# Where VectorE evacuates the last block: six weight splits placed ahead of it

## The chip, the cores and the metric

The kernel runs on one core of a Trainium2 chip. The metric is the device time of one execution in microseconds (us). Engines are named as in the profile: PE (TensorE), PEld (its weight loads), DVE (VectorE), ACT (ScalarE), POOL (GpSimd), SP (SyncE, which here only issues DMAs). Each engine runs its own instruction stream in order and waits on semaphores that others raise.

## The reference, cut to what matters

One layer over 512 tokens of width 1024, float32: a mixer (retention and differential attention), a routed mixture of 16 experts with two experts for each token, and a gated embedding. The change lies where the mixture ends and the gated embedding begins:

```python
for gi in range(N_GROUPS):
    sl = slice(gi * EXPERTS_PER_GROUP, (gi + 1) * EXPERTS_PER_GROUP)
    hid = jax.nn.silu(jnp.einsum('td,edf->etf', t, w_gate[sl])) * jnp.einsum('td,edf->etf', t, w_up[sl])
    hid = hid * combine[:, sl].T[:, :, None]       # routing weights, zero for all but two experts
    out = out + jnp.einsum('etf,efd->td', hid, w_down[sl])
...
x = x + out                                        # out as returned by the mixture
gate = jax.nn.sigmoid(rmsnorm(x, norm_ple[i]) @ w_ple_gate[i])
x = x + gate * (p[i] @ w_ple_proj[i])
return rmsnorm(x, norm_final)
```

## The kernel before, in words

The tokens are four tiles of 128 rows. The mixture sorts the 1024 pairs of token and expert by expert and cuts them into blocks of 64 pairs; in this execution there are 23 blocks. For each block POOL gathers the rows, PE multiplies by gate and up weights (L1556), ACT and DVE make the hidden values, PE transposes them and multiplies by the down weights (L1580) into a PSUM bank. DVE copies that bank to SBUF (`evacuate_y`, L1209), and POOL scatters the copy to `y_rows` in HBM (L657 copies a column of row numbers, L677 issues the indirect DMA). The blocks run in a loop; the last block is finished behind the loop by code of its own.

After the mixture comes what the code calls stage 6. SP waits until the scatter of the last block has landed, and then gathers the two expert rows of every token into `yg`, tile by tile, in eight DMAs of 512 KB (L633). DVE waits for the two of tile 0 and adds them, weighted, to the residual `xr` (`stage6_a`, L1242 and L1243). PE transposes the sum (L1610), ACT rounds it to a high part `x2T_hi` (L897), DVE forms the low part `x2T_lo` (L1250), and PE multiplies by the gate weights in three passes (high by high, low by high, high by low: L1296 to L1298). ACT, DVE and SP finish each tile behind PE.

The gate weights themselves are prepared in between. SP loads them as one DMA of 4 MB (`ple_gate_raw`, L627). ACT makes sixteen high pieces of 128x512 (`ple_hi`, L887), each raising `pg_hi`. DVE makes sixteen low pieces (`split_gate`, L1229): piece n waits for `pg_hi` to reach n + 1, subtracts, and raises `pg_lo`. PE's gate products wait for eight of them per half. The high and low pieces of the first half lie in buffers of ring slot 2, which the next to last expert has left; `yg` lies in the slot of the last expert.

On DVE the order is written out by hand: the hidden values of the last block, its evacuation, the splits, then stage 6. These lines set it:

```python
hiddenT(last_block)                        # L1234: waits for PE's transposes
evacuate_y(last_block, 2, fresh=True)      # L1235: waits dn_done(last), copies, raises y_ready
split_gate(range(2 * KD))                  # L1236: sixteen pieces (KD is 8)
```

POOL's last scatter (L693) waits for the `y_ready` of that copy, SP waits for the scatter's landing (L629), and the first wait of `stage6_a(0)` (L1241) is for the gathers.

Of the kernel before, what the change touches and what calls it, by code (L numbers as in the profile page):

```python
# [39 lines left out]
KD = D // P  # L40
# [161 lines left out]
def trunk(nc, x, p, norm_mix, w_in, lam_q1, lam_k1, lam_q2, lam_k2, diff_subln, w_out, norm_ffn,  # L202
# [3 lines left out]
    with ctx:  # L206
# [721 lines left out]
        def _(dve):  # L928
# [268 lines left out]
            def hiddenT(b):  # L1197

                dve.wait_ge(hT_done, b + 1)
                V.tensor_copy(hidT[:], b_hT[:, 0:256].rearrange("p (j q t) -> p j q t", j=2, q=2)).then_inc(hidT_ready, 1)  # L1200
# [3 lines left out]
            def evacuate_y(b, buf, fresh=False):  # L1204
                dve.wait_ge(dn_done, b + 1)
                if not fresh:

                    dve.wait_ge(s_ystored, 16 * b)
                V.tensor_copy(y_blk[buf][:], b_dn[:]).then_inc(y_ready, 1)  # L1209
# [14 lines left out]
            def split_gate(pieces):  # L1224

                for n in pieces:
                    q, k = n // KD, n % KD
                    dve.wait_ge(pg_hi, n + 1)
                    V.scalar_tensor_tensor(ple_lo[q][:, k, :], ple_gate_raw[:, k, q * HALF:(q + 1) * HALF],  # L1229
                                           gple[:, k:k + 1], ple_hi[q][:, k, :].bitcast(F32), ALU.mult,  # L1230
                                           ALU.subtract).then_inc(pg_lo, 1)


            hiddenT(last_block)  # L1234
            evacuate_y(last_block, 2, fresh=True)  # L1235
            split_gate(range(2 * KD))  # L1236


            def stage6_a(i):
# [413 lines left out]
```

## Time and profile before

| what | value |
|---|---|
| median of 3 runs | 661.52 us (661.12 to 661.74) |
| the profiled execution's own time | 661.52 us |
| its span | 659.7 us |
| mean granted clock of TensorE | 0.968 |
| PE busy | 614.5 us, 93% of the span |
| DVE busy | 215.6 us, 33% |
| ACT busy | 202.3 us, 31% |
| POOL busy | 59.8 us, 9% |

The span is from the first to the last instruction in the trace; the execution's time has 1.8 us more around it. Slices of the page are a fortieth of the span, 16.5 us each. A granted clock of 1.00 is TensorE's upper level, 2.4 GHz, and 0.50 the lower one, 1.2 GHz. Times inside the trace count from the span's start.

### The profile page before, as it was taken

The numbers are of one execution on the slowest core, as the hardware profiler recorded it, in microseconds if no ns is written. First come the engines' busy times: TensorE is split into PE (matmuls) and PEld (weight loads), VectorE is DVE, ScalarE is ACT, GpSimd is POOL, SyncE is SP. The second block draws the span as 40 slices with busy tenths as digits, with TensorE's granted clock in tenths as the row PEclk, the third lists the DMA queues.
The fourth block names the chain that finished last, engine by engine and source line by source line (L and its number), as shares of the span: only waits on it lengthen the run. The fifth ranks groups of instructions, "written<-read, shape, count | busy, mean of one in ns | idle before, by whom it ended". The sixth has DMA issues, their size and how long they took to land.

```text
span 659.7 us, 9372 instructions
## 1 busy us (share of the span) xinstructions
PE 614.5 (93%) x3378; PEld 389.2 (59%) x3379; DVE 215.6 (33%) x480; ACT 202.3 (31%) x440; POOL 59.8 (9%) x105
## 2 busy tenths in 40 slices
PE   6999999999999999996899999999999999935995
PEld 6998877879989899953233333333333333314883
DVE  3521265456253442365011110111111011165663
ACT  5532354545444533342110100101010010152674
POOL 0000000000000000002112212121221212110000
PEclk8999999999999999978899999999999999986998
DMA  8743114111111079854989999998998999955001
GB/s 311 210 153 128 64 65 128 64 65 65 65 65 65 1 262 393 311 224 155 330 322 398 398 394 397 382 343 294 395 397 326 379 399 396 406 217 204 32 33 64
DMA packets 76416, 153.34 MB, mean 232 GB/s; under 512 B 7960, under 2 KB 27296, under 8 KB 76128
## 3 DMA queue, kind: packets, MB, share of 16 engines
q1 hardware_dynamic: 72144, 139.77, 57.8%
q0 software_dynamic: 3952, 12.85, 5.1%
q8 instruction: 22, 0.36, 0.2%
q10 hardware_dynamic: 288, 0.28, 0.2%
q14 instruction: 10, 0.08, 0.0%
HBM read 142.66 MB, written 10.23 MB: 232 GB/s over the span
## 4 chain that ended last, share of the span: by engine, by line
PE 85%; DVE 5%; DMA 4%; ACT 2%; SPq 2%; issue 2%; DVEq 0%; POOLq 0%; POOL 0%; ACTq 0%
PE bank L1556 22%; PE bank L1296 13%; PE bank L1297 12%; PE bank L1298 12%; PE bank L1580 11%; PE bank L1378 2%; DMA ring_gu<-in_w_up 2%; PE bank L1503 2%; PE bank L1544 2%; SPq L577 2%; PE bank L1351 2%; DVE ple_lo L1229 2%; DMA gmix<-in_norm_mix 1%; PE bank L1568 1%; PE bank L1392 1%
## 5 line engine op out<-in xcount | busy, mean ns | idle before, releaser
L1556 PE MATMUL bank<-ring_gu,rowsT 128*64 128x512 f32 x736 | 165.2, 601 | 2.8 <-issue 1.7
L1556 PEld LDWEIGHTS bank<-ring_gu,rowsT 128*64 128x64 f32 x736 | 51.0, 138 | 100.8 <-issue 99.6
L1580 PE MATMUL bank<-ring_dn,hidT 128*64 128x512 f32 x368 | 84.0, 598 | 1.4 <-DVE hidT L1200 1.4
L865 ACT ACTIVATE silu_g<-bank 128x256 f32<-128x256 f32 x23 | 8.8, 383 | 236.5 <-PE bank L1556 236.5
L1045 DVE TENSOR_TENSOR w_lo<-w_raw,w_hi 128x2048 fp32r<-128x2048 f32 x18 | 41.3, 2292 | 76.8 <-ACT w_hi L730 69.6
L1195 DVE TENSOR_TENSOR hid<-silu_g,bank 128x256 f32<-128x256 f32 x23 | 9.7, 421 | 166.0 <-ACT silu_g L865 166.0
L1296 PE MATMUL bank<-w_hi,hT_hi 128*128 128x256 f32 x192 | 56.1, 292 | 0.8 <-issue 0.8
L1297 PE MATMUL bank<-w_lo,hT_hi 128*128 128x256 f32 x192 | 54.9, 286 | 0.0
L1298 PE MATMUL bank<-w_hi,hT_lo 128*128 128x256 f32 x192 | 54.8, 286 | 0.0
L1296 PE MATMUL bank<-hT_hi,w_hi 128*128 128x512 f32 x128 | 50.8, 397 | 0.0
L1580 PEld LDWEIGHTS bank<-ring_dn,hidT 128*64 128x64 f32 x368 | 24.4, 136 | 44.7 <-issue 44.7
L1297 PE MATMUL bank<-hT_lo,w_hi 128*128 128x512 f32 x128 | 49.9, 390 | 0.0
L1298 PE MATMUL bank<-hT_hi,w_lo 128*128 128x512 f32 x128 | 49.9, 390 | 0.0
L1209 DVE COPY y_blk<-bank 128x512 f32<-128x512 f32 x23 | 15.9, 692 | 78.1 <-PE bank L1580 78.1
L1296 PEld LDWEIGHTS bank<-w_hi,hT_hi 128*128 128x128 f32 x192 | 37.5, 195 | 2.1 <-issue 2.1
L1297 PEld LDWEIGHTS bank<-w_lo,hT_hi 128*128 128x128 f32 x192 | 37.5, 195 | 0.0
L1298 PEld LDWEIGHTS bank<-w_hi,hT_lo 128*128 128x128 f32 x192 | 37.4, 195 | 0.0
L730 ACT ACTIVATE w_hi<-w_raw 128x2048 fp32r<-128x2048 f32 x18 | 34.3, 1906 | 2.1 <-DMA w_raw<-in_w_in 2.1
L657 POOL COPY src_now<-src_row 128x1 int32 (+1 forms) x26 | 5.2, 199 | 312.6 <-DVE dst_row L1023 304.2
L1296 PEld LDWEIGHTS bank<-hT_hi,w_hi 128*128 128x128 f32 x128 | 24.0, 188 | 8.0 <-issue 3.3
L1296 PE MATMUL bank<-ple_hi,x2T_hi 128*128 128x512 f32 x64 | 26.0, 407 | 2.5 <-issue 2.5
L665 POOL DMA_INDIRECT rows<-h_rows,src_now x26 | 25.7, 990 | 20.7 <-POOL src_now L657 20.7
(210 smaller groups left out, 906.5 us busy)
## 6 DMA issues: line engine op xcount, KB each, us to landing
ring_gu<-in_w_gate SPq DMA_DIRECT2D x32, 1024.0 KB, 14.4
ring_gu<-in_w_up SPq DMA_DIRECT2D x32, 1024.0 KB, 15.3
ring_dn<-in_w_down SPq DMA_DIRECT2D x16, 2048.0 KB, 14.0
w_raw<-in_w_in SPq DMA_DIRECT2D x14, 1024.0 KB, 5.0
w_raw<-in_w_out SPq DMA_DIRECT2D x4, 1024.0 KB, 4.8
ple_gate_raw<-in_w_ple_gate SPq DMA_DIRECT2D x1, 4096.0 KB, 26.3
yg<-y_rows SPq DMA_DIRECT2D x8, 512.0 KB, 7.5
xr<-in_x SPq DMA_DIRECT2D x4, 512.0 KB, 9.2
```

Source lines behind the costliest of these rows:

```text
L577: sp.dma_start(ring_gu[slot][:, ks, n, :], src[:, ks, :]).then_inc(s_gu[slot][half], 16)
L665: pool.indirect_dma_start(out=rows[buf][:], out_offset=None, in_=h2_rows, in_offset=rows_of).then_inc(s_rows[buf], 16)
L730: nc.scalar.activation(w_hi[u % 2][:], w_raw[u % 2][:], ACT.Copy).then_inc(hi_done, 1)
L1045: V.tensor_tensor(w_lo[u % 2][:], w_raw[u % 2][:], w_hi[u % 2][:].bitcast(F32), ALU.subtract).then_inc(lo_done, 1)
L1209: V.tensor_copy(y_blk[buf][:], b_dn[:]).then_inc(y_ready, 1)
L1229: V.scalar_tensor_tensor(ple_lo[q][:, k, :], ple_gate_raw[:, k, q * HALF:(q + 1) * HALF], gple[:, k:k + 1], ple_hi[q][:, k, :].bitcast(F32 ...
L1296: T.matmul(o, w_of(w[0], k), m_of(m[0], k), start=(k == 0), stop=False)
L1297: T.matmul(o, w_of(w[0], k), m_of(m[1], k), start=False, stop=False)
L1298: last = T.matmul(o, w_of(w[1], k), m_of(m[0], k), start=False, stop=(k == KD - 1))
L1351: last = T.matmul(b_score[2 * (i % 2) + c][:, 0:L], dqT[64 * c:64 * c + 64, h, i * P:(i + 1) * P], dkT[64 * c:64 * c + 64, h, 0:L], start= ...
L1556: last = T.matmul(b_gu[q * BLK:(q + 1) * BLK, :], rowsT[:, k % 4, k // 4, :], ring_gu[s][:, k, :, q * UC:(q + 1) * UC], start=(k == 0), st ...
L1580: last = T.matmul(b_dn[q * BLK:(q + 1) * BLK, :], hidT[:, kf % 2, kf // 2, :], ring_dn[s][:, kf, q * (D // 2):(q + 1) * (D // 2)], start=( ...
```

## The change

The sixteen pieces of `split_gate` are issued in two groups: pieces 0 to 5 before the evacuation of the last block, pieces 6 to 15 after it. No instruction is added or removed, and none of another engine moves.

```diff
             hiddenT(last_block)
+            split_gate(range(6))
             evacuate_y(last_block, 2, fresh=True)
-            split_gate(range(2 * KD))
+            split_gate(range(6, 2 * KD))
```

The functions that it calls stay as they are:

```python
def evacuate_y(b, buf, fresh=False):
    dve.wait_ge(dn_done, b + 1)
    ...
    V.tensor_copy(y_blk[buf][:], b_dn[:]).then_inc(y_ready, 1)

def split_gate(pieces):
    for n in pieces:
        q, k = n // KD, n % KD
        dve.wait_ge(pg_hi, n + 1)
        V.scalar_tensor_tensor(ple_lo[q][:, k, :], ple_gate_raw[:, k, q * HALF:(q + 1) * HALF],
                               gple[:, k:k + 1], ple_hi[q][:, k, :].bitcast(F32), ALU.mult,
                               ALU.subtract).then_inc(pg_lo, 1)
```

## Rows read from the trace of the kernel before

**Rows 1.** The page: PE's busy tenths in 40 slices of the span.
```profile
PE   6999999999999999996899999999999999935995
```

**Rows 2.** Chain that ended last, 580 to 606: start us, us, what.
```profile
581.18 3.67 PE bank L1580 x16
...
585.57 8.70 DVE ple_lo L1229 x14
...
596.17 1.21 DVE xr L1242
...
598.74 1.98 PE bank L1610 x8
...
603.25 0.76 PE bank L1296
```

**Rows 3.** Timeline of DVE, 579 to 600: start, duration, what, idle before.
```profile
584.88 0.69 DVE L1209 COPY y_blk<-bank 128x512 f32<-128x512 f32 x1 [3.83 <-PE bank L1580]
...
596.09 1.28 DVE L1242 SCALAR_TENSOR_TENSOR xr<-yg,w_top,xr 128x1024 f32<-128x1024 f32 x1
```

**Rows 4.** Lines L1229 and L887: ns min/median/max, first and last start us.
```profile
L1229 DVE SCALAR_TENSOR_TENSOR ple_lo<-ple_gate_raw,gple,ple_hi x16: 741/745/746, 585.5 to 595.4; 128x512 fp32r<-128x512 f32 x16
L887 ACT ACTIVATE ple_hi<-ple_gate_raw,gple x16: 704/706/721, 584.2 to 593.4; 128x512 fp32r<-128x512 f32 x16
```

**Rows 5.** Timeline of ACT, its first split of the gate weights.
```profile
584.21 0.72 ACT L887 ACTIVATE ple_hi<-ple_gate_raw,gple 128x512 fp32r<-128x512 f32 x1 [7.73 <-DMA ple_gate_raw<-in_w_ple_gate]
```

**Rows 6.** Timeline of SP: the gate weights' load, the eight gathers.
```profile
557.35 2.02 SPq L627 DMA_DIRECT2D ple_gate_raw<-in_w_ple_gate  x1
590.18 4.58 SPq L633 DMA_DIRECT2D yg<-y_rows  x8
```

**Rows 7.** Line L627, the gate weights' load: time to landing.
```profile
DMA to landing us min/median/max: 26.3/26.3/26.3
```

**Rows 8.** Timeline of POOL, 579 to 589: the last two scatters.
```profile
580.50 0.18 POOL L657 COPY dst_now<-dst_row 128x1 int32 x1 [7.58 <-DVE y_blk L1209]
581.50 1.00 POOL L677 DMA_INDIRECT y_rows<-y_blk,dst_now  x1 [0.82 <-POOL dst_now L657]
585.82 0.45 POOL L657 COPY dst_now<-dst_row 128x1 int32 x1 [3.32 <-DVE y_blk L1209]
587.10 1.32 POOL L677 DMA_INDIRECT y_rows<-y_blk,dst_now  x1 [0.83 <-POOL dst_now L657]
```

**Rows 9.** Line L677: the scatter at 587.10, its time to landing.
```profile
DMA to landing us min/median/max: 3.1/3.1/3.1
```

**Rows 10.** Timeline of SP, the second gather of tile 0.
```profile
590.56 0.43 SPq L633 DMA_DIRECT2D yg<-y_rows  x1
```

**Rows 11.** Line L633: that second gather, its time to landing.
```profile
DMA to landing us min/median/max: 4.6/4.6/4.6
```

**Rows 12.** Line L633, all eight gathers: time to landing.
```profile
DMA to landing us min/median/max: 3.7/7.5/9.9
```

**Rows 13.** Timeline of DVE, 601 to 608: the sum of tile 1.
```profile
604.58 1.27 DVE L1242 SCALAR_TENSOR_TENSOR xr<-yg,w_top,xr 128x1024 f32<-128x1024 f32 x1
```

**Rows 14.** Stretches: busy us by engine, granted clock, DMA share, GB/s.
```profile
557.00:583.60 26.60, 25.21 (x120) 8.51 (x118) 3.46 (x8) 1.96 (x4) 5.93 (x10) 1.00 1.02 397
589.80:598.70 8.90, 0.00 (x0) 0.00 (x0) 8.85 (x12) 4.31 (x8) 0.00 (x0) 0.50 0.81 286
603.20:606.80 3.60, 3.55 (x8) 2.81 (x9) 2.26 (x3) 1.26 (x2) 0.00 (x0) 0.50 0.02 5
606.80:651.00 44.20, 44.20 (x208) 36.83 (x207) 24.21 (x40) 26.57 (x47) 0.00 (x0) 1.00 0.10 36
```

**Rows 15.** Timeline of PE, an earlier resumption of long matmuls.
```profile
287.70 7.93 PE L1503 MATMUL bank<-ple_proj,pT 128*128 128x512 f32 x12 [0.69 <-ACT pT L843]
```

**Rows 16.** Stretches behind that resumption, columns as in Rows 14.
```profile
287.70:292.70 5.00, 5.00 (x6) 2.18 (x7) 4.15 (x28) 2.26 (x4) 0.00 (x0) 0.50 0.39 147
292.80:300.00 7.20, 7.20 (x21) 3.49 (x20) 3.50 (x15) 2.25 (x4) 0.00 (x0) 1.00 1.04 391
```

## The prediction

> **What bounds the kernel now.** I read the page first: PE is busy in almost every slice; thin are the first, two in the middle, the fifth and fourth from the end (3 and 5 tenths) and the last [rows 1]. The pair of 3 and 5 is the seam between the mixture and stage 6, and the change lies there. The chain of waits through the seam reads: the last down product on PE, from 581.18 to 584.85; the evacuation; the splits of line L1229; DVE's sum of tile 0 at 596.17; PE's transposes at 598.74; the first gate product at 603.25 [rows 2]. From 606.8 to 651.0 PE is busy 44.20 of 44.20 us at the upper clock level [rows 14]. So the kernel ends a fixed time after the gate products start, and those start a fixed time after DVE's sum of tile 0. A microsecond that this sum starts later is a microsecond at the end, as long as nothing that runs behind PE takes over.
>
> That sum starts at 596.09 in DVE's timeline [rows 3], and two things must be there first. One is DVE itself: sixteen splits, the last started at 595.4 [rows 4]. The other is the data: evacuation, scatter, gathers. The chain names only the later one, the splits. The whole question is how far behind it the other one lies.
>
> **The slack of the data.** The evacuation starts at 584.88 [rows 3]. POOL begins its column copy at 585.82 and its scatter at 587.10 [rows 8]; the scatter lands 3.1 later [rows 9], at 590.2, and SP issues the first gather at 590.18 [rows 6]. The second gather of tile 0 is issued at 590.56 [rows 10] and lands 4.6 later [rows 11], at 595.16. From the start of the evacuation to the data of tile 0 it is 595.16 - 584.88 = 10.28 us. DVE takes the data at 596.09, so this path has only 0.93 us of slack.
>
> **When six splits can run.** Before the change DVE is idle for 3.83 us ahead of the evacuation [rows 3]. That looks like free room for six splits, but a split needs ACT's high piece. ACT's first piece starts at 584.21 and takes 0.72 [rows 5], so it is ready at 584.93, after PE has finished the last down product (584.85). The idle stretch is over by then. ACT started there because it waited for the load of the gate weights [rows 5]: issued at 557.35 [rows 6], landed 26.3 later [rows 7], at 583.65, in a stretch in which the DMA engines were full at 397 GB/s [rows 14].
>
> Step by step, after the change:
> 1. DVE starts split 0 at about 584.96, 0.03 behind ACT's piece, as the evacuation started 0.03 behind PE (581.18 + 3.67 = 584.85 to 584.88) [rows 2, 3].
> 2. Splits come at a pace of (595.4 - 585.5) / 15 = 0.66 us by their first and last start [rows 4]. ACT makes its pieces faster, one in (593.4 - 584.2) / 15 = 0.61 us [rows 4], so DVE doesn't wait for it again. Six splits are 6 x 0.66 = 3.96 us.
> 3. The evacuation starts at 584.96 + 3.96 = 588.92 instead of 584.88, that is 4.04 us later.
> 4. What is queued behind it: DVE's other ten splits, POOL's last scatter, SP's gathers behind the landing of that scatter. POOL and SP have nothing else left to do. The order evacuation, split, split is met again by POOL, so its times are taken over, and the data of tile 0 lands at 588.92 + 10.28 = 599.20.
> 5. DVE's work has the same sum. It started with the evacuation at 584.88 and starts now with a split at 584.96, so it is done at 596.09 + 0.08 = 596.2, and then waits 3 us for the gathers.
> 6. The sum of tile 0 starts at 599.20 + 0.03 = 599.23. The path that sets it changes over from the splits to the gathers, and the loss is 599.23 - 596.09 = 3.14 us: the delay of 4.04 less the slack of 0.93, and 0.03 for the release.
>
> What could soften it later: nothing that I find. The gathers of the tiles 1 to 3 move by 4.04 and their users by 3.14. Tile 1's are the third and fourth of eight that are issued over 4.58 us [rows 6], so by 592.5, and with the longest landing of all, 9.9 [rows 12], they are in by 602.4, after the change by 606.4; tile 1 is summed at 604.58 [rows 13], after the change at 607.7. The later tiles have a tile's worth of PE work more. PE's transposes, ACT's rounding and the first products follow DVE's sum in the same order, so the same 603.25 - 596.09 = 7.16 us [rows 2, 3] lies between. The gate products wait for all low pieces of their half too; those are done at 596.2 in both orders.
>
> The sum: the profiled execution took 661.52 us, its span 659.7 and 1.8 around it, and the median of the three runs is the same 661.52. So 661.52 + 3.14 = **664.7 us**.
>
> **The sizes that no row gives exactly.** POOL's share depends on what DVE does beside it. In the scatter of the block before, with DVE still, the copy took 0.18 and the scatter 1.00; the last ones took 0.45 and 1.32 beside the splits [rows 8]. If POOL met no split this would be 0.27 + 0.32 = 0.6 us less; if twice as much got in its way, 0.6 more. I take the last scatter's own times, since DVE still runs splits behind the evacuation.
>
> The Trainium skill (SBUF — State Buffer, section "Who interferes with whom") says that a DVE instruction with two SBUF inputs contends with a GpSimd one that reads SBUF, and the one that comes second waits for the whole instruction. The last copy bears that out: it ended at 585.82 + 0.45 = 586.27, and the split beside it, begun at 585.49 with 0.745 us, at 586.23 [rows 4, 8]. By that rule the copy may wait up to one whole split, 0.5 us more than it did, and the time would be 665.2.
>
> TensorE's clock is the other one. The granted clock falls to the lower level in PE's idle stretch and is 0.50 from 589.8 [rows 14]; PE idles until 598.74 before and until 601.9 after, so nothing is new in kind. It rises at 606.8, 3.55 us after the first gate product. At an earlier place, long matmuls resumed at 287.70 [rows 15] and the level rose only by 292.8, 5.1 us later [rows 16]. In a slow stretch half the time is lost: if the after kernel needs 5.1 instead of 3.55, it pays (5.1 - 3.55) / 2 = 0.8 us. If the rise came at the first product, it would gain 3.55 / 2 = 1.8; no resumption in these rows shows that, and half of it, 0.9, is my lower bound.
>
> The Trainium skill (TensorE: Matmul & The Clock Gate, Part 1, "What's actually happening") says the same kernel can show different numbers of slow matmuls, since the chip's sampling doesn't start with the kernel. The two resumptions differ as it says; by it a shift of the start by 3.1 us may move this term either way.
>
> **The rivals.**
> - *The six splits fill the idle 3.83 us* (faster). Place: DVE between 581.05 and 584.88. It happens if the gate weights land early enough for ACT. If they land L us earlier, the evacuation is late by 4.04 - L only, and DVE is done L earlier. At L = 3.83 split 0 starts at 581.13, the evacuation at 585.1, tile 0 is in at 595.4, and the gain is 596.1 - 595.4 = 0.7 us: 660.8. It decides at 4.04 - L below 0.93, so L above 3.1, a load of under 23.2 instead of 26.3 us. For it: the load is one DMA, and ACT was ready for it 7.7 us earlier. Against it: the DMA engines are full all through it [rows 14], and the change moves no DMA.
> - *The gathers hide* (no change, 661.5). Their path would have to be 3.1 us shorter than its 10.28, which leaves nearly no time for one of its parts: scatter 3.1, gathers 4.6. That holds too if the order written were not the order run, which the in-order timeline of DVE speaks against.
> - *The clock comes back late* (slower still). As worked out, 0.8 us on top: 665.5.
> - *POOL meets no split*: 664.1, inside the forecast's own kind.
>
> **How the numbers follow.** The forecast, with POOL's variants, gets 0.81; the late clock 0.12; no change 0.03; the faster one 0.04. Unknown costs reach from 3.14 - 0.6 - 0.9 = 1.6 to 3.14 + 0.6 + 0.8 = 4.5 us; each end needs two things at once. The runs before lie within 0.4 below and 0.2 above their median. From these the range is 663.0 to 666.2 (1.5 and 4.7 over 661.5), which leaves out the rivals of the other signs and little else. A measurement of this kernel can tell about 0.2% (1.3 us) from no change. Slower by more than that: 0.93, from the first two cases. Within it: 0.03. Faster: 0.04 in name, but a gain of 0.7 us would itself be under 1.3, so most of it counts as no change: 0.06 same, 0.01 faster.
>
> **What would show it.** In the changed kernel's profile: six pieces of L1229 starting at 585.0, each 0.66 apart, and the copy of L1209 at about 588.9; POOL's last scatter at 591.2; SP's first gather at 594.2; DVE idle for about 3 us, ended by a DMA of `yg`, ahead of L1242 at 599.2; the chain through the seam naming the scatter and the gathers in place of the splits; PE's idle stretch 17 instead of 13.9 us; the busy stretch of 44.2 us the same in length. Steps 1 to 3 are wrong if the evacuation starts before 588; the slack is wrong if the sum of tile 0 is late by much other than 3.1 us while the evacuation is late by 4.0; the forecast fails if the sum starts before 597.5.

## The result, and the profile after

| | kernel before | changed kernel |
|---|---|---|
| median of 20 runs | 661.47 us (657.0 to 662.46) | 664.55 us (660.04 to 665.88) |
| ratio to before, 95% interval | | 1.0052 (1.0036 to 1.0067) |
| profiled execution, span | 659.7 us | 658.4 us |

The changed kernel is slower by 3.1 us by the medians and by 2.4 to 4.4 us by the interval (0.0036 and 0.0067 of 661.5). The forecast was 664.7. The shortest executions of the two kernels, 657.0 us (three of the twenty) and 660.1 (two of the twenty), lie 3.1 us apart too.

One thing has to be set aside before the traces are laid side by side: the changed kernel's profiled execution is *shorter* than that of before. Its last down product ends 4.14 us earlier. In this profile TensorE keeps its upper clock level through the routing of the mixture, near 290 us, where the profile of before has the lower one for a time. The stretch 286.5 to 300 shows it, first before, then after (the last numbers are the granted clock, the DMA share and GB/s):

```profile
286.50:300.00 13.50, 12.81 (x29) 5.78 (x28) 8.66 (x49) 5.44 (x10) 0.00 (x0) 0.77 0.79 299
```

```profile
286.50:300.00 13.50, 13.45 (x39) 6.46 (x39) 11.38 (x52) 5.54 (x10) 0.00 (x0) 1.00 0.84 291
```

This stretch is not the whole difference. The profiles with one split ahead and with two loads and six ahead (below) keep the level there too, yet their last down products end at 584.15 and 584.13, only 0.7 us earlier than before. In those two the level is lower in the first blocks: 0.50 from 310 to 315 us and 0.72 to 0.73 from 320 to 325, against 0.83 and 1.00 in the changed kernel. All of it lies more than 250 us ahead of the seam. No profile was taken of a short execution of the kernel before, so that these have the same cause is not shown.

So the seam is read against an event inside it, the end of PE's last down product: 581.18 + 3.65 = 584.83 before (the chain gives 584.85 for the same end), 577.04 + 3.65 = 580.69 after. DVE, ACT and PE at the seam of the changed kernel, from its timelines (start, duration, engine, line; in brackets the idle time ahead and its releaser); these lines answer to [rows 3], [rows 5] and the PE rows of [rows 2]:

```profile
580.75 4.06 DVE L1229 SCALAR_TENSOR_TENSOR ple_lo<-ple_gate_raw,gple,ple_hi 128x512 fp32r<-128x512 f32 x6 [3.85 <-ACT ple_hi L887]
584.73 0.68 DVE L1209 COPY y_blk<-bank 128x512 f32<-128x512 f32 x1
585.33 6.70 DVE L1229 SCALAR_TENSOR_TENSOR ple_lo<-ple_gate_raw,gple,ple_hi 128x512 fp32r<-128x512 f32 x10
595.07 1.28 DVE L1243 SCALAR_TENSOR_TENSOR xr<-yg,w_top,xr 128x1024 f32<-128x1024 f32 x1 [3.03 <-DMA yg<-y_rows]
```

```profile
579.99 2.56 ACT L887 ACTIVATE ple_hi<-ple_gate_raw,gple 128x512 fp32r<-128x512 f32 x4 [7.66 <-DMA ple_gate_raw<-in_w_ple_gate]
```

```profile
577.04 3.65 PE L1581 MATMUL bank<-ring_dn,hidT 128*64 128x512 f32 x16 [1.39 <-DVE hidT L1200]
597.73 1.97 PE L1611 MATMUL bank<-small,xr 128*128 128x128 f32 x8 [17.04 <-DVE xr L1244]
602.24 0.77 PE L1297 MATMUL bank<-ple_hi,x2T_hi 128*128 128x512 f32 x1 [2.54 <-issue]
```

DVE waits 3.85 us for ACT, as long as it waited for PE before; the idle time was not filled. Six splits follow, the evacuation starts 4.04 us behind the down product instead of 0.05, and DVE then stands still for 3.03 us ahead of the sum, which it never did before. PE's idle stretch grows from 13.90 to 17.04. The sum lies 11.26 us behind the down product in the kernel before, and 11.25 to 11.26 in the three other kernels below that put no split ahead, so a difference of a tenth in this distance can be read from single profiles. The chain through the seam now names the way of the data (start, us, what), where [rows 2] had the splits:

```profile
584.81 0.61 DVE y_blk L1209
...
585.69 0.44 POOL dst_now L657
...
586.95 3.07 DMA y_rows<-y_blk,dst_now
...
590.42 4.56 DMA yg<-y_rows
...
595.07 1.30 DVE xr L1243
```

POOL's last copy and scatter are as they were, 0.45 and 1.32 us, to be held against [rows 8]:

```profile
585.66 0.45 POOL L657 COPY dst_now<-dst_row 128x1 int32 x1 [7.31 <-DVE y_blk L1209]
586.95 1.32 POOL L677 DMA_INDIRECT y_rows<-y_blk,dst_now  x1 [0.83 <-POOL dst_now L657]
```

And the clock comes back 3.0 us after the first gate product, where [rows 14] has 3.6 (columns as there):

```profile
602.20:605.20 3.00, 2.96 (x7) 2.43 (x8) 1.67 (x3) 1.25 (x2) 0.00 (x0) 0.50 0.04 14
605.20:650.00 44.80, 44.80 (x210) 37.09 (x209) 24.80 (x40) 26.56 (x47) 0.00 (x0) 1.00 0.10 36
```

The spans now add up: 659.7, less 584.83 - 580.69 = 4.14 for the earlier last product, plus 3.12 for the sum of tile 0 (14.38 us behind the product instead of 11.26), less (3.57 - 2.96) / 2 = 0.3 for the shorter slow stretch, is 658.4, the measured span.

### The profile page after: what moved, and what is told of

Same layout as the page of the kernel before. It is cut to its first block, busy times and chain, and to the rows that moved or that the text cites. A ratio compares the mean times of both kernels' runs of the same rounds, so it can differ in the third digit from the quotient of the medians.

```text
span 658.4 us, 9372 instructions
## 1 busy us (share of the span) xinstructions
PE 609.9 (93%) x3378; PEld 386.6 (59%) x3379; DVE 215.6 (33%) x480; ACT 201.9 (31%) x440; POOL 59.8 (9%) x105
## 4 chain that ended last, share of the span: by engine, by line
PE 80%; DMA 9%; DVE 4%; ACT 2%; SPq 2%; issue 2%; POOLq 0%; DVEq 0%; POOL 0%; ACTq 0%
PE bank L1557 20%; PE bank L1297 13%; PE bank L1298 12%; PE bank L1299 12%; PE bank L1581 10%; DMA ple_gate_raw<-in_w_ple_gate 4%; PE bank L1379 2%; DMA ring_gu<-in_w_up 2%; PE bank L1504 2%; PE bank L1545 2%; SPq L577 2%; PE bank L1352 2%; DMA gmix<-in_norm_mix 1%; PE bank L1393 1%; PE bank L1569 1%
```

## The experiments

In all of them the seam is measured as above, from the end of the last down product in their own profile. The table is worked out from the starts in the timelines:

| kernel | evacuation | sum of tile 0 | evacuation to sum | DVE idle ahead of the sum | slow gate products | median, us |
|---|---|---|---|---|---|---|
| before, none ahead | 0.05 | 11.26 | 11.21 | 0 | 3.57 | 661.4 to 661.5 |
| one ahead | 0.75 | 11.28 | 10.53 | 0 | 3.0 | 661.11 |
| three ahead | 2.03 | 12.33 | 10.30 | 1.00 | 5.4 | 663.32 |
| six ahead (the change) | 4.04 | 14.38 | 10.34 | 3.03 | 3.0 | 664.55 |
| sixteen ahead | 10.67 | 20.42 | 9.75 | 9.07 | 4.4 | 671.54 |
| two loads, none ahead | 0.04 | 11.25 | 11.21 | 0 | 3.2 | 660.56 |
| two loads, six ahead | 0.10 | 10.47 | 10.37 | 3.06 | 3.8 | 660.44 |
| the same, DVE kept from POOL | 0.10 | 10.37 | 10.27 | 1.79 | 3.6 | 660.63 |

The columns evacuation and sum count in us from the end of the down product; slow gate products is the time from the first gate product until the clock level rises. Each median belongs to a set of executions of its own, beside the kernel before, and the ratios given below are to that one.

### How the loss grows with the number of splits ahead

```diff
-            split_gate(range(6))
+            split_gate(range(n))           # n = 1, 3 or 16
             evacuate_y(last_block, 2, fresh=True)
-            split_gate(range(6, 2 * KD))
+            split_gate(range(n, 2 * KD))
```

One ahead:

> One split ahead of the last evacuation. Theory (slack of 0.93 us): the evacuation is 0.08 + 0.66 = 0.74 us later, which is inside the slack; the data is in 0.2 us before DVE is done, the sum of tile 0 starts 0.08 later than before, with DVE not idle ahead of it, and the time is 661.5. Rival (each split ahead costs its duration): 662.2.

Three ahead:

> Splits 0 to 2 ahead of the last evacuation instead of 0 to 5. Theory (the data path evacuation, scatter, gathers sets the sum of tile 0, with 0.93 us of slack): the evacuation is 0.08 + 3 x 0.66 = 2.06 us later than before, the sum of tile 0 starts 10.3 us behind the evacuation, DVE idles 1.1 us ahead of it, and the time is 661.5 + 1.15 = 662.6. Rival (any split ahead costs its full duration, no slack): 661.5 + 2.06 = 663.6. Rival (cost is that of the wait for ACT, whatever the number of splits): 664.6 as with six.

All sixteen ahead:

> All sixteen splits ahead of the last evacuation. Theory: the evacuation is 0.08 + 16 x 0.66 = 10.6 us later than before, less the slack of 0.93: the sum of tile 0 starts 9.7 us later, and the time is 671.2. POOL then meets no split, so the path from evacuation to data should be shorter than 10.28: by 0.6 us if both the copy (0.45 back to 0.18) and the scatter (1.32 back to 1.00) speed up, which gives 670.6. Rival (DVE's work is what counts, the order costs one constant): 664.6. Rival (POOL's slower last copy and scatter come from the code behind the loop, not from the splits beside them): 0.45 and 1.32 stay, 671.2.

DVE's sum of tile 0 in the three, in this order:

```profile
595.43 1.28 DVE L1243 SCALAR_TENSOR_TENSOR xr<-yg,w_top,xr 128x1024 f32<-128x1024 f32 x1
```

```profile
596.32 1.28 DVE L1243 SCALAR_TENSOR_TENSOR xr<-yg,w_top,xr 128x1024 f32<-128x1024 f32 x1 [1.00 <-DMA yg<-y_rows]
```

```profile
606.35 1.28 DVE L1242 SCALAR_TENSOR_TENSOR xr<-yg,w_top,xr 128x1024 f32<-128x1024 f32 x1 [9.07 <-DMA yg<-y_rows]
```

With one ahead nothing is paid: 0.02 us at the sum for 0.70 at the evacuation, and DVE is not idle; the ratio is 0.9994 (0.9970 to 1.0018). From three on, every microsecond of the evacuation is paid in full: from three to six 2.01 at the evacuation and 2.05 at the sum. The slack that follows is the delay of the evacuation less that of the sum: 1.98 - 1.07 = 0.91 from three, 3.99 - 3.12 = 0.87 from six; 0.93 was read before. A rival without slack would have 0.7 at one, one with a constant cost would have the same at three and at sixteen; both fall. Three ahead was timed 1.0045 (1.0028 to 1.0062), that is 1.9 to 4.1 us, more than the 1.15 us expected. By the time alone, 663.32 us, the rival without slack (663.6) would fit better; it falls by the seam, where the sum is 1.07 us later and not 2. The rest of the 1.9 us between the medians could be the clock's: in the profile the gate products ran slow for 5.4 us instead of 3.6, which is 0.9 us. That the other executions did the same is not shown, and up to the 3.0 us of the ratio another 1.0 us is left open:

```profile
603.50:608.80 5.30, 5.30 (x13) 4.19 (x14) 2.63 (x3) 1.20 (x2) 0.00 (x0) 0.50 0.04 12
608.90:650.00 41.10, 41.10 (x195) 34.23 (x194) 23.21 (x39) 26.56 (x47) 0.00 (x0) 1.00 0.10 39
```

With sixteen ahead the ratio is 1.0144 (1.0113 to 1.0176, from six executions), or 9.5 us, where 9.1 to 9.7 were expected; the sum is 9.16 later. No split runs beside POOL, and its last copy and scatter take the times of the blocks before:

```profile
597.53 0.18 POOL L657 COPY dst_now<-dst_row 128x1 int32 x1 [13.94 <-DVE y_blk L1209]
598.54 0.99 POOL L677 DMA_INDIRECT y_rows<-y_blk,dst_now  x1 [0.83 <-POOL dst_now L657]
```

The way from evacuation to sum is 9.75 instead of 10.34 us, the 0.6 that the prediction put on the splits. The rival that blamed the code behind the loop falls with it.

### Would the six splits pay if their input were there?

```diff
-            sp.dma_start(ple_gate_raw[:], w_ple_gate...).then_inc(s_plegate, 16)
+            for q in range(2):
+                sp.dma_start(ple_gate_raw[:, :, q * HALF:(q + 1) * HALF],
+                             w_ple_gate...[:, :, q * HALF:(q + 1) * HALF]).then_inc(s_pghalf[q], 16)
...
-            act.wait_ge(s_plegate, 32)
+            act.wait_ge(s_plegate, 16)          # the other load on this semaphore
             act.wait_ge(dn_done, ...)
             for q in range(2):
+                act.wait_ge(s_pghalf[q], 16)
                 for k in range(KD):
```

> The changed order (six splits ahead), and the gate weights loaded as two DMAs of 2 MB, one for each half of the columns, each with a semaphore of its own; ACT waits for the first alone before its first eight pieces. Theory: the first half lands near 578.4 on the scale of the kernel before (half of the bytes at 397 GB/s is 5.3 us ahead of 583.65), ACT starts behind the last but one down product near 580, and six splits fill DVE's idle 3.83 us; the evacuation starts at 585.0, the sum of tile 0 at 595.3 instead of 596.09, DVE idle ahead of it; 660.8, 0.75 under the kernel before and 3.9 under the changed one. Rival (a split ahead of the evacuation costs its duration whenever the high pieces are ready): 664.6. Rival (the two smaller DMAs land later than the one): above 661.5.

> The order of the kernel before (no split ahead), with the gate weights loaded as the same two DMAs of 2 MB. Theory: DVE idles as before until the evacuation at 584.88, the splits still end at 596.1 and set the sum of tile 0; 661.5, as the kernel before. Rival (the earlier load alone is what helps): 660.8, as with six splits ahead.

DVE and ACT with two loads and six splits ahead:

```profile
580.26 4.06 DVE L1234 SCALAR_TENSOR_TENSOR ple_lo<-ple_gate_raw,gple,ple_hi 128x512 fp32r<-128x512 f32 x6
584.23 0.68 DVE L1214 COPY y_blk<-bank 128x512 f32<-128x512 f32 x1
584.83 6.71 DVE L1234 SCALAR_TENSOR_TENSOR ple_lo<-ple_gate_raw,gple,ple_hi 128x512 fp32r<-128x512 f32 x10
594.60 1.28 DVE L1248 SCALAR_TENSOR_TENSOR xr<-yg,w_top,xr 128x1024 f32<-128x1024 f32 x1 [3.06 <-DMA yg<-y_rows]
```

```profile
578.77 9.91 ACT L892 ACTIVATE ple_hi<-ple_gate_raw,gple 128x512 fp32r<-128x512 f32 x16 [3.00 <-PE bank L1586]
```

ACT now waits for a down product and no longer for the load, and starts 5.36 us ahead of the end of the last one instead of 0.62. DVE goes from the hidden values straight into the splits; they end as PE does, and the evacuation starts 0.10 behind it. The sum comes at 10.47 instead of 11.26, 0.79 us earlier, with 0.75 expected. The same two loads without the splits ahead leave it at 11.25. So neither edit gains alone: the splits ahead need the earlier load, and the earlier load needs the splits ahead. In time neither is clear of no change: 0.9982 (0.9963 to 1.0001) with six ahead, 0.9990 (0.9974 to 1.0006) with none; the 0.79 us is shown by the seams of single profiles.

### Keeping DVE away from POOL

```diff
             scatter(total - 1, 2, 2 * total + ROW_BUFS)
+            pool.sem_inc(last_scatter, 1)
...
             evacuate_y(last_block, 2, fresh=True)
+            dve.wait_ge(last_scatter, 1)
             split_gate(range(6, 2 * KD))
```

> As the kernel with the gate weights in two DMAs and six splits ahead, and DVE waits behind the evacuation until POOL has issued the last scatter (a semaphore of its own that POOL raises behind it), so that no split runs beside POOL's copy and scatter. Theory: copy 0.18 and scatter 1.00 as with all splits ahead, evacuation to sum 9.75 instead of 10.34 us; the ten splits left run from 3.0 behind the evacuation for 6.6 us and end about when the data is in; the sum of tile 0 starts 0.5 to 0.6 us earlier than with early6, 0.5 under its time. Rival (the splits become the last to end, since the wait takes 3 us from them): DVE not idle ahead of the sum and no gain, or a loss of some tenths.

It missed its aim. The profile of it, POOL and then DVE:

```profile
581.94 0.18 POOL L662 COPY dst_now<-dst_row 128x1 int32 x1 [3.29 <-DVE y_blk L1216]
582.96 1.44 POOL L682 DMA_INDIRECT y_rows<-y_blk,dst_now  x1 [0.83 <-POOL dst_now L662]
```

```profile
582.78 6.71 DVE L1236 SCALAR_TENSOR_TENSOR ple_lo<-ple_gate_raw,gple,ple_hi 128x512 fp32r<-128x512 f32 x10 [1.09 <-POOLq L699]
591.28 1.28 DVE L1251 SCALAR_TENSOR_TENSOR xr<-yg,w_top,xr 128x1024 f32<-128x1024 f32 x1 [1.79 <-DMA yg<-y_rows]
```

The copy took its short 0.18, but POOL's sequencer raised the semaphore behind the scatter before the scatter had begun to show as work: DVE's splits start at 582.78, the scatter at 582.96, and the scatter takes 1.44 instead of 1.00. The way from evacuation to sum is 10.27, 0.1 under the kernel with two loads and six ahead, where 0.5 to 0.6 were expected. The time is 0.9992 (0.9969 to 1.0015) of before. A wait that keeps DVE still until the scatter is really over was not tried.

### What TensorE's clock takes in the seam

```diff
             down(total - 1)
+            for n in range(13):
+                T.matmul(b_gate[1][0][:], ones[:], ple[:, 0, 0:HALF], start=True, stop=True)
```

> The kernel before, with thirteen matmuls of 128x512 in float32 on PE behind the last down product, into a PSUM bank that tile 1's gate product overwrites later; their result is not used. It sizes the clock's part of the seam. Theory: the clock stays at the upper level, the eight transposes take 0.87 instead of 1.98 us, the first gate product starts 1.1 us earlier against DVE's sum, and the slow stretch of 3.57 us behind it (1.8 us lost) is gone: 658.6. DVE, POOL and the gathers keep their times. Rival (the level falls in the gap that is left, or the matmuls run past the sum of tile 0): 661.5 or more.

It gave 1.0000 (0.9979 to 1.0021) where 2.9 us less were expected, a clear miss. Busy time and granted clock in three stretches of it:

```profile
585.00:599.10 14.10, 11.55 (x33) 5.23 (x31) 13.14 (x19) 8.52 (x14) 1.44 (x2) 1.00 0.63 227
599.30:601.80 2.50, 0.04 (x1) 0.00 (x0) 1.29 (x2) 2.40 (x5) 0.00 (x0) 0.50 1.00 411
601.90:606.00 4.10, 4.10 (x10) 3.27 (x11) 2.63 (x3) 1.19 (x2) 0.00 (x0) 0.50 0.07 28
```

The level holds through the thirteen matmuls and the gap of 2.55 us behind them. It falls at 599.2, near the end of the transposes (598.23 to 599.34), and stays down through a second gap of 2.54 us. The transposes are fast (sum to first gate product 6.30 instead of 7.16), but the gate products then run slow for 4.1 us. With the two loads, six splits ahead and DVE kept from POOL as above, the same thirteen matmuls gave:

> The two DMAs for the gate weights, six splits ahead, DVE quiet until the last scatter is issued, and the thirteen matmuls on PE, all together. Theory: the terms add, 0.75 + 0.55 + 2.9 = 4.2 us under the kernel before: 657.3. Rival (with a shorter idle stretch the thirteen matmuls run into the transposes): 0.5 to 1 more.

0.9976 (0.9956 to 0.9996), 660.05 us. It was expected at 657.3. In its profile the level held through a gap of 1.88 us, the transposes and a gap of 2.54, fell at 598.6, 0.5 us after the first gate product, and rose at 602.0. The transposes are fast again (6.30 us from the sum to the first gate product), but the gate products are slow for 3.4 us: most of the gain that was expected of the clock isn't there either. The next pair fills the gaps:

```diff
-            for n in range(13):
+            for n in range(15):                # 14 with the two loads
...
             x2_transpose(0)
+            for n in range(2):
+                T.matmul(b_gate[1][0][:], ones[:], ple[:, 0, 0:HALF], start=True, stop=True)
```

> The kernel before with fifteen matmuls of 128x512 (0.88 us each, from the thirteen in 11.43 us of warm0) behind the last down product, which leaves about 0.8 us of gap before the transposes of tile 0, and two more behind those transposes, which fill 1.8 of the 2.5 us until the first gate product. Theory (warm0 lost its gain because the level fell in the gaps of 2.5 us around the transposes): with the gaps filled the level stays up; the sum of tile 0 to the first gate product takes 6.3 us as in warm0 instead of 7.16, and the gate products start at full speed, which saves the 3.57 / 2 = 1.8 us of before; 661.5 - 2.6 = 658.9. Rival (the level falls for another reason than the gaps): slow gate products of 3 to 5 us as before, 660.6 to 661.5.

> The gate weights in two DMAs with six splits ahead (early6), with fourteen matmuls behind the last down product and two behind the transposes of tile 0. Theory: the two terms add, 0.75 + 2.6 = 3.4 us under the kernel before: 658.1, and 6.5 under the changed kernel. Rival: as in warm2, the level falls all the same, 659.9 to 660.8.

The kernel before with the gaps filled:

```profile
585.00:599.10 14.10, 13.27 (x35) 5.84 (x34) 13.48 (x19) 8.86 (x15) 1.78 (x2) 1.00 0.61 232
599.30:602.20 2.90, 2.09 (x8) 0.80 (x7) 1.29 (x2) 2.48 (x5) 0.00 (x0) 1.00 0.92 374
602.20:606.00 3.80, 3.79 (x17) 3.13 (x18) 2.50 (x3) 1.22 (x2) 0.00 (x0) 1.00 0.01 3
```

The level stays up, and the time is 658.50 us, 0.9953 (0.9934 to 0.9972). With the two loads and six ahead it is 657.96 us, 0.9937 (0.9917 to 0.9957), the fastest version of this study, 3.4 us under the kernel before and, against another set of executions, 6.6 under the changed one by the medians. In its profile POOL's last copy waited for the landing of the scatter before it, and the evacuation to sum is 11.02 instead of 10.37 us. The sum lies 11.12 us behind the down product, against 11.26 before: of the 0.79 us that the splits ahead had gained, 0.14 are left. So the two gains did not add in this profile:

```profile
585.33 0.68 POOL L661 COPY dst_now<-dst_row 128x1 int32 x1 [3.73 <-DMA y_rows<-y_blk,dst_now]
```

## Why the prediction was right

The term that the number hangs on is shown: the sum of tile 0 moved by 3.12 us where 3.14 were worked out. That the medians moved by 3.1 as well is closer than the interval (2.4 to 4.4 us) can tell, and in part luck, since the clock's term varies by up to 1.2 us between profiles.

- **Where the splits can start** (steps 1 and 2). As forecast: ACT's first piece is ready about when PE is done, and DVE idles 3.85 us ahead of the first split. Six splits and the hand-over put the evacuation 3.99 us later than before (4.04 less 0.05); 4.04 were forecast.
- **The way of the data** (steps 3 and 4). 10.28 us were read from the evacuation to the landing, 10.31 to the sum. After the change it is 10.34, with all parts as they were: the scatter landed 3.07 after its start, the second gather 4.56.
- **The slack** (step 6). 0.93 us was the term that made 4.04 into 3.14. The sum of tile 0 is 3.12 later, and the series of one, three, six and sixteen splits shows the corner between one and three, with a slack of 0.87 to 0.91.
- **DVE's own work** (step 5). Its ten later splits end near 592.0, 3.03 us ahead of the data; 3 were forecast.
- **The rival on the faster side** was a true mechanism whose condition was not met; with the load cut in two it happened in the seam, at 0.79 us, where 0.7 was worked out.
- **POOL beside the splits.** The 0.6 us were the splits' doing, and remained, as taken. The Trainium skill's rule (SBUF — State Buffer, "Who interferes with whom"), that a GpSimd instruction reading SBUF waits out a DVE one with two SBUF inputs, agrees with the copy: 0.18 without splits, 0.45 beside them in the changed kernel, ending when a split ends. How much the copy waits depends on where in a split it falls: in the fastest kernel it took 0.68, and with thirteen matmuls added it began at 585.65, as one split followed another, and took 0.18 beside them. The whole split of waiting that the prediction allowed for was not met. The scatter is longer beside splits too, 1.25 to 1.45 against 0.99 and 1.00 alone; what it waits for is not shown.
- **The clock.** The late rise that was bounded at 0.8 us was met in one profile, at 0.9 (5.4 us with three ahead), not in the changed kernel's (3.0 us). The slow part of the gate products lies between 3.0 and 5.4 us over the profiles with no matmuls added, in no order of the splits ahead. It spreads the times; in the changed kernel's profile it is shorter than before, so it explains none of that profile's loss.

## What to carry to other kernels

Idle time ahead of an instruction can be filled only by work whose inputs are there by then: look up the producer's first finish, not the length of the gap. When an in-order engine sets off a chain of copies and DMAs, that hand-off goes first, and bulk work goes behind it; behind it the bulk here ended only 0.93 us after the data, and ahead of it it cost its whole length, less those 0.93 us of slack. Read that slack as the difference between the two things a step waits for; the chain that ended last names only one of them.

## What the runs showed of the hardware

With thirteen matmuls added, TensorE's level held at 1.00 through 11.43 us of matmuls and a gap of 2.55, and fell at 599.2, when PE had been busy again for 1.0 us. In the second kernel with thirteen it held through a gap of 1.88, fell 0.5 us after the end of a gap of 2.54, and was low for 3.4 us of gate products. With fifteen and two added the gaps were 0.83 each, with fourteen and two 1.57 and 0.83, and it stayed up. The Trainium skill (TensorE: Matmul & The Clock Gate, Part 1, "What's actually happening") lets the level fall only after idle time. That agrees in so far as a gap stood ahead of each fall; both falls showed when PE was already busy again, behind pauses shorter than PE's idle stretch of 13.9 us.

The semaphore that POOL raises behind an indirect DMA released DVE 0.2 us before that DMA's instruction began in the trace, in both kernels that have it (582.78 against 582.96, and 583.12 against 583.29). The trace names POOLq, POOL's sequencer, as the releaser, and not the DMA's instruction. POOL's spans are rough, but as far as the trace shows, this semaphore doesn't tell that POOL has done with the DMA.
